# The last stick-breaking head feeds TensorE float32 values directly, without the split into a rounded and a low part

## What is computed

```python
z = einsum('bhqd,bhkd->bhqk', qb, kh[:, :, :end]) * scale
strict = s_pos < t_pos
log_beta = log_sigmoid(z)
log_1m = where(strict, -softplus(z), 0.0)
suffix = cumsum(log_1m, axis=3, reverse=True) - log_1m
a = where(strict, exp(log_beta + suffix), 0.0)
outs.append(einsum('bhqk,bhkd->bhqd', a, vh[:, :, :end]))
```

## Time and profile before

| | |
|---|---|
| median of 3 runs | 1202.79 us |
| the three runs | 1201.45, 1202.79, 1959.26 us |
| the profiled execution | 1201.39 us, span 1199.5 us |
| TensorE busy | 1161.3 us, 97% |
| DVE, ACT, POOL busy | 47%, 47%, 48% |

### The profile page before, as it was taken

One profiled execution on the slowest core, in us unless ns is written; L12 is line 12 of the kernel. 1 busy time (PEld: TensorE's weight loads), 2 busy tenths in 40 slices (PEclk: granted clock), 3 DMA queues, 4 the chain that ended last, 5 costly groups with the idle time before them and its releaser, 6 DMA issues.

```text
span 1199.5 us, 15304 instructions
## 1 busy us (share of the span) xinstructions
PE 1161.3 (97%) x5566; PEld 973.9 (81%) x5566; DVE 559.8 (47%) x760; ACT 569.7 (47%) x834; POOL 572.2 (48%) x292
## 2 busy tenths in 40 slices
PE   7999998989999999999999999899999999999996
PEld 5888887878888888888888889687888888888885
DVE  7756677766222222222455666768642222222225
ACT  5778887444233223133446878855331422322421
POOL 3535563574434444444644645447554444444450
PEclk9999998999999999999999999999999999999998
DMA  5212110322332323322221211112332232232322
GB/s 185 73 51 70 37 36 19 105 87 90 108 101 90 105 87 105 97 96 88 92 84 53 71 36 55 51 36 71 123 106 99 95 97 97 87 105 87 105 71 71
DMA packets 30153, 99.63 MB, mean 83 GB/s; under 512 B 3728, under 2 KB 5776, under 8 KB 30096
## 3 DMA queue, kind: packets, MB, share of 16 engines
q1 hardware_dynamic: 29664, 98.33, 24.7%
q10 hardware_dynamic: 432, 0.55, 0.1%
HBM read 96.77 MB, written 2.10 MB: 82 GB/s over the span
## 4 chain that ended last, share of the span: by engine, by line
PE 83%; ACT 4%; DVE 3%; issue 2%; POOL 2%; POOLq 2%; DMA 1%; DVEq 1%; SPq 0%; ACTq 0%
PE DW L418 23%; PE DW L420 23%; PE DW L419 23%; POOL w L905 2%; PE Z L563 2%; PE Z L570 2%; PE Z L552 1%; DMA raw<-in_weights 1%; PE DW L508 1%; PE O L582 1%; POOLq L913 1%; PE Z L418 1%; PE Z L420 1%; PE Z L419 1%; PE O L532 1%
## 5 line engine op out<-in xcount | busy, mean ns | idle before, releaser
L905 POOL TENSOR_TENSOR w<-raw,w 128x1024 fp32r<-128x1024 f32 x178 | 431.8, 2427 | 384.3 <-ACT w L675 380.0
L675 ACT ACTIVATE w<-raw 128x1024 fp32r<-128x1024 f32 x177 | 185.8, 1052 | 216.9 <-PE DW L420 195.6
L418 PE MATMUL DW<-xm,w 128*128 128x512 f32 x512 | 201.0, 393 | 5.1 <-POOL w L905 5.1
L420 PE MATMUL DW<-xm,w 128*128 128x512 f32 x512 | 199.9, 390 | 0.0
L419 PE MATMUL DW<-xm,w 128*128 128x512 f32 x512 | 199.8, 390 | 0.0
L418 PE MATMUL DW<-stage,w 128*128 128x512 f32 x512 | 199.5, 390 | 0.0
L420 PE MATMUL DW<-stage,w 128*128 128x512 f32 x512 | 199.2, 389 | 0.0
L419 PE MATMUL DW<-stage,w 128*128 128x512 f32 x512 | 199.2, 389 | 0.0
L1224 DVE TENSOR_TENSOR kf<-o 128x512 f32<-128x512 f32 x64 | 65.2, 1019 | 196.7 <-ACT o L856 196.5
L1240 DVE TENSOR_TENSOR DW<-DW,probs 128x512 f32<-128x512 f32 x62 | 43.4, 699 | 222.9 <-PE DW L420 222.9
L418 PE MATMUL DW<-xa,w 128*128 128x512 f32 x296 | 119.9, 405 | 7.8 <-DVE xa L1013 7.8
(11 more groups left out here) (216 smaller groups left out, 1644.5 us busy)
## 6 DMA issues: line engine op xcount, KB each, us to landing
raw<-in_weights SPq DMA_DIRECT2D x179, 512.0 KB, 3.3
out_x<-x SPq DMA_DIRECT2D x16, 128.0 KB, 1.9
x<-in_x SPq DMA_DIRECT2D x6, 256.0 KB, 6.3
raw<-in_weights SPq DMA_DIRECT2D x2, 256.0 KB, 4.8
x<-in_x ACTq DMA_DIRECT2D x2, 256.0 KB, 5.4
work<-in_positions SPq DMA_DIRECT2D x1, 256.0 KB, 6.8
gains<-in_gains ACTq DMA_DIRECT2D x1, 28.0 KB, 3.9
inv_freq<-in_inv_freq SPq DMA_DIRECT2D x1, 0.5 KB, 7.1
```

Source lines behind the costliest of these rows:

```text
L418: pe.matmul(bank, w[:, slot, 0, k], rhs[:, 0, c], start=start, stop=False)
L420: mm = pe.matmul(bank, w[:, slot, 1, k], rhs[:, 0, c], start=False, stop=stop)
L675: act.activation(w[:, slot_of(at_layer), 0], raw[:, p % 2], ACT.Identity).then_inc(w_hi, 1)
L905: pool.tensor_tensor(w[:, slot, 1], raw[:, p % 2], w[:, slot, 0].bitcast(F32), ALU.subtract).then_inc(w_ready, 1)
```

## The change

In head 7 alone, BX reads `work` itself as float32, once, in place of `sp` hi and lo, and BA reads `work` itself in place of `at` hi and lo. The constants and the values are read as float32 too. The steps BH7, BL7, XH7 and XL7 are gone, and the counts that other waits use are adapted (seven splits in a layer, not eight). BX7 now waits for BP7, and BA7 for XE7. A wait of BH7 for BX6 goes with it. Both order tables are written anew: in layer 1 almost only the four steps drop out, in layer 0 more of them stand in another place.

```diff
 BX:
-pe.wait_ge(sb_split, l * SB_HEADS + n + 1)
+if n == LAST_HEAD:
+    pe.wait_ge(sb_sp, l * SB_HEADS + n + 1)
+    parts = [work[:, n % 2]]
+    tri, one = minus_tri[:, :].bitcast(F32), minus_one[:, :].bitcast(F32)
+else:
+    pe.wait_ge(sb_split, l * SPLIT_HEADS + n + 1)
+    parts = [sp[:, 0], sp[:, 1]]
+    tri, one = minus_tri[:, :], minus_one[:, :]
 for j in (0, 1, 3, 2):
-    for f in range(2):
-        pe.matmul(Z[n][:, Z_AT[j]:Z_AT[j] + Z_LEN[j]], minus_tri[:, :],
-                  sp[:, f, Z_AT[j]:Z_AT[j] + Z_LEN[j]],
...
+    for part in parts:
+        pe.matmul(Z[n][:, Z_AT[j]:Z_AT[j] + Z_LEN[j]], tri, part[:, Z_AT[j]:Z_AT[j] + Z_LEN[j]],
...
 BA:
-pe.wait_ge(sb_alo, l * SB_HEADS + n + 1)
+if n == LAST_HEAD:
+    pe.wait_ge(z_drained, l * SB_HEADS + n + 2)
+    parts, v = [work[:, n % 2]], vst.bitcast(F32)
+else:
+    pe.wait_ge(sb_alo, l * SPLIT_HEADS + n + 1)
+    parts, v = [at[:, 0], at[:, 1]], vst
...
 BH:
 act.wait_ge(sb_sp, l * SB_HEADS + n + 1)
-if n == LAST_HEAD:
-    act.wait_ge(zx_full, l * SB_HEADS + n)
 act.activation(sp[:, 0], work[:, n % 2], ACT.Identity).then_inc(sb_hi, 1)
...
 ORDER_0, last lines:
-BP7 BH7 BD5 BL7 OS0 CH21 XH6 GH2 OS1 GL2 XL6 OS2 BX7 OE0 CL20 BA6 XE7 BO6 OS3 XH7 BD6 XL7 OE1 CL21 OE2 OS4
-CH22 CL22 BA7 BO7 OS5 BD7 CH23 OE3 CL23 GH3 CH24 CL24 OS6 OS7 NS0 GL3 NSE0 OE4 OE5 NSD0 NSF0 OE6 OE7
+BO5 BP7 OS1 BD5 CH21 GL1 GH2 XL6 OS2 BX7 OE0 CL20 OE1 BA6 XE7 BO6 OS3 BD6 BA7 OS4 CH22 OE2 CL21 CL22 BO7 BD7
+CH23 OE3 CL23 GH3 OS5 CH24 OS6 CL24 NS0 GL2 OE4 GL3 NSE0 OS7 OE5 NSD0 NSF0 OE6 OE7
```

More of the change, by code:

```diff
@@ L93 @@
 LAST_HEAD = SB_HEADS - 1
+SPLIT_HEADS = SB_HEADS - 1
 ORDER_0 = """
[L113 to L126, removed]
@@ L127 @@
-BP7 BH7 BD5 BL7 OS0 CH21 XH6 GH2 OS1 GL2 XL6 OS2 BX7 OE0 CL20 BA6 XE7 BO6 OS3 XH7 BD6 XL7 OE1 CL21 OE2 OS4
-CH22 CL22 BA7 BO7 OS5 BD7 CH23 OE3 CL23 GH3 CH24 CL24 OS6 OS7 NS0 GL3 NSE0 OE4 OE5 NSD0 NSF0 OE6 OE7
+T0 U0 AG0 T1 CH3 AG1 NP0 NA0 NAE0 AG2 NAD0 T2 AG3 CL3 NAF0 TE0 AG4 U1 AG5 AG6 TH0 AG7 CH4 U2 TL0 TE1 TE2 AG8
+CL4 AG9 CH5 T3 AG10 TH1 AG11 TL1 U3 RE2 CL5 SN0 RM2 TE3 T4 RS2 RE3 RA2 RS3 U4 TH2 RM3 T5 CH6 TL2 RA3 TE4 TH3
+CL6 VT4 VH4 TL3 CH7 BS0 BE0 U5 VL4 T6 TE5 RE5 BP0 CL7 RM5 RS5 U6 RA5 BH0 TH5 BL0 TE6 CH8 BX0 TL5 WS0 VT6 XE0
@@ new lines @@
+CH9 WM0 BS1 T7 WE0 CL8 VH6 WR0 WN0 WT0 U7 WH0 WL0 BE1 TE7 TH7 WS1 VL6 WM1 T8 U8 WE1 BP1 BH1 CH10 WR1 CL9 WN1
+WA0 XH0 WO0 XL0 TL7 TE8 BL1 WT1 WH1 T9 WL1 WS2 WD0 CH11 TH8 BX1 WA1 WM2 WE2 XE1 WO1 TL8 U9 WR2 WD1 CL10 WN2
+BS2 CL11 CH12 TE9 WT2 WH2 RE9 BA0 T10 WL2 RM9 BO0 RS9 WS3 BE2 BD0 RA9 TH9 WM3 U10 WA2 CL12 CH13 TL9 WE3 XH1
+T11 WO2 BP2 WR3 TE10 U11 BH2 RE10 BL2 WN3 RM10 RS10 XL1 TE11 CH14 RA10 TH10 WT3 BX2 CL13 VT11 SQ0 BA1 WH3 WD2
+SQ1 WL3 XE2 TL10 VH11 BO1 BS3 WS4 BD1 BE3 WM4 T12 WE4 CL14 WA3 WO3 U12 BP3 WR4 WN4 WT4 VL11 XH2 BH3 WH4 TE12
@@ new lines @@
+WD3 WL4 BL3 T13 WS5 CH15 WA4 XL2 WM5 CL15 TH12 BX3 WE5 TL12 WR5 U13 WO4 SA0 WN5 TE13 T14 CH16 WD4 WT5 XE3 TH13
+BA2 TL13 SQ2 BS4 WH5 CL16 SA1 WL5 WS6 XH3 BE4 WM6 BO2 XL3 WE6 BD2 CH17 BP4 T15 U14 SA2 WA5 BH4 WR6 TE14 U15
+BL4 SQ3 WN6 WT6 TH14 WO5 WH6 BX4 CH18 TE15 WD5 WL6 WS7 TL14 VT15 BA3 SQ4 XE4 WM7 BO3 BS5 BD3 T16 SA3 CL17 VH15
+SQ5 WE7 SA4 CL18 WA6 BE5 VL15 WO6 WR7 WN7 U16 WT7 WD6 T17 BP5 XH4 XL4 WH7 WL7 BH5 SQ6 SA5 BL5 WA7 TE16 SA6
+CH19 WO7 WD7 U17 CH20 TH16 TE17 GH0 BX5 GL0 SQ7 XE5 SA7 NW0 CL19 TL16 NWE0 NWD0 NWF0 BS6 MN0 BA4 BE6 MH0 MN1
@@ L129 @@
+MN2 VT17 BS7 GH1 BP6 BH6 ML0 XH5 MN3 MH1 VH17 BL6 MH2 BO4 VL17 BX6 XL5 BD4 MH3 BA5 ML1 ML2 BE7 XE6 ML3 XH6 OS0
+BO5 BP7 OS1 BD5 CH21 GL1 GH2 XL6 OS2 BX7 OE0 CL20 OE1 BA6 XE7 BO6 OS3 BD6 BA7 OS4 CH22 OE2 CL21 CL22 BO7 BD7
+CH23 OE3 CL23 GH3 OS5 CH24 OS6 CL24 NS0 GL2 OE4 GL3 NSE0 OS7 OE5 NSD0 NSF0 OE6 OE7
 """
@@ L143 @@
 XE5 NW0 NWE0 TL17 GH0 BS6 NWD0 CL20 BE6 GH1 NWF0 GL0 MN0 BA4 CH21 MN1 BP6 BH6 MH0 XH5 MN2 MH1 MN3 BO4 BS7 BL6
-ML0 XL5 BD4 MH2 ML1 MH3 BX6 ML2 BE7 ML3 BA5 OS0 XE6 OS1 BP7 BH7 OS2 BL7 OE0 GL1 XH6 BX7 XL6 BO5 OE1 OS3 BD5
-XE7 BA6 OE2 BO6 CL21 XH7 OS4 BD6 OE3 OS5 XL7 GH2 CH22 OE4 BA7 OS6 CL22 BO7 BD7 OE5 GH3 GL2 OS7 GL3 NS0 OE6
-CH23 CH24 NSE0 OE7 NSD0 CL23 CL24 NSF0
+ML0 XL5 BD4 MH2 ML1 MH3 BX6 ML2 BE7 ML3 BA5 OS0 XE6 OS1 BP7 OS2 OE0 GL1 XH6 BX7 XL6 BO5 OE1 OS3 BD5 XE7 BA6
+OE2 BO6 CL21 OS4 BD6 OE3 OS5 GH2 CH22 OE4 BA7 OS6 CL22 BO7 BD7 OE5 GH3 GL2 OS7 GL3 NS0 OE6 CH23 CH24 NSE0 OE7
+NSD0 CL23 CL24 NSF0
 """
@@ L558, in _ @@
                     elif step == "BX":
-                        pe.wait_ge(sb_split, l * SB_HEADS + n + 1)
+                        if n == LAST_HEAD:
[6 more added lines that the diff above has]
+                            tri, one = minus_tri[:, :], minus_one[:, :]
                         for j in (0, 1, 3, 2):
-                            for f in range(2):
-                                pe.matmul(Z[n][:, Z_AT[j]:Z_AT[j] + Z_LEN[j]], minus_tri[:, :],
-                                          sp[:, f, Z_AT[j]:Z_AT[j] + Z_LEN[j]],
-                                          start=False, stop=j == NB - 1 and f == 1, skip_group_check=True)
+                            for part in parts:
+                                pe.matmul(Z[n][:, Z_AT[j]:Z_AT[j] + Z_LEN[j]], tri, part[:, Z_AT[j]:Z_AT[j] + Z_LEN[j]],
+                                          start=False, stop=j == NB - 1 and part is parts[-1], skip_group_check=True)
                         for j in range(NB - 1):
@@ L568, in _ @@
                                 at0 = Z_AT[j] + P * (jj - j)
[L569 to L572, removed]
+                                for part in parts:
+                                    mm = pe.matmul(Z[n][:, at0:Z_AT[j] + Z_LEN[j]], one,
+                                                   part[:, Z_AT[jj]:Z_AT[jj] + Z_LEN[jj]], start=False,
+                                                   stop=jj == NB - 1 and part is parts[-1], skip_group_check=True)
                         mm.then_inc(zx_full, 1)
                     elif step == "BA":
-                        pe.wait_ge(sb_alo, l * SB_HEADS + n + 1)
+                        if n == LAST_HEAD:
[4 more added lines that the diff above has]
+                            parts, v = [at[:, 0], at[:, 1]], vst
                         pe.wait_ge(o_drained, l * O_USES + plan.o_use[step, n] + 1)
@@ L580, in _ @@
                         for j in range(NB):
[L581 to L584, removed]
+                            for part in parts:
+                                mm = pe.matmul(O[:, j * P:T], v[:, n // 2 % 2, j, n % 2, :],
+                                               part[:, Z_AT[j]:Z_AT[j] + Z_LEN[j]],
+                                               start=j == 0 and part is parts[0],
+                                               stop=j == NB - 1 and part is parts[-1])
                         mm.then_inc(o_full, 1)
@@ L782, in _ @@
                         if n > 1:
-                            act.wait_ge(sb_alo, l * SB_HEADS + n - 1)
+                            act.wait_ge(sb_alo, l * SPLIT_HEADS + n - 1)
                         act.activation(work[:, n % 2], Z[n], ACT.Abs)
@@ L1138, in _ @@
                     elif step == "BL":
-                        dve.wait_ge(sb_hi, l * SB_HEADS + n + 1)
+                        dve.wait_ge(sb_hi, l * SPLIT_HEADS + n + 1)
                         dve.tensor_tensor(sp[:, 1], work[:, n % 2], sp[:, 0].bitcast(F32), ALU.subtract
```

8 lines of the change are left out of this document (4 added, 4 removed).

## The result

The changed kernel takes 1204.4 us (median of 20 runs, 1203.31 to 1205.19), the kernel before 1201.49 us in runs on the same chip (median of 20, from 1199.7). The ratio is 1.0024, with a 95% interval of 1.0018 to 1.003: about 2.9 us slower. One run of the kernel before took 1959.26 us; it is left out of the comparison, and what delayed it isn't known. The profiled execution of the changed kernel took 1203.89 us.

The account below looks back on a forecast made before the run. TensorE, busy 1161.3 of 1199.5 us, was taken as the bound. Layer 1's +2.5 and layer 0's -0.6 us gave 1203.3 us on the profiled 1201.39, 1204.7 on the median 1202.79; forecast 1204 us, 8-in-10 range 1199.5 to 1208.5.

Parts of the forecast that it names:

- Removed steps, zero: Head 7's four split steps on ACT, DVE and POOL: removing them ends no TensorE wait, zero, at most 1.6 us.
- Float32 products, +2.5 us a layer: BX7 and BA7 on TensorE: at 1.68 ns a column they grow by 1.58 and 0.94 us in each layer.
- The dear end for small products: 128-column float32 products in BX7 and BA7 might each cost as much as 256-column ones: 1.1 us more.
- Layer 1, +2.5 us, rigid: Layer 1 behind BA7: everything moves by 2.5 us, and the 1.94 us pause ahead of the MLP stays.
- Layer 0, -0.6 us, as 1.0 - 1.56: Layer 0: MLP starts 1.0 us later, pause shrinks from 3.13 to 1.6 us, and a kept-up clock saves 1.56 us.
- The pause of 1.94 us doesn't drop the clock, that of 3.13 us does: TensorE's clock behind the pause ahead of the MLP: with 1.6 us, layer 0 should match layer 1, saving 1.56 us.
- The early reorder of layer 0, zero with 1.6 us to either side: The other rearranged steps of ORDER_0: short groups change places where TensorE hardly waits, zero, bounds 1.6 us either way.
- Rival 1: Layer 0's pause absorbs nothing, pack 26 moves with TensorE, clock falls: 1206.4 or 1207.8 us, up to 1209; chance 0.24.
- Rival 2: Layer 0's new order removes the short waits and the clock stays up: 1200 to 1202.5 us; chance 0.16.
- Rival 3: A float32 product on TensorE costs only what the two parts cost, so no added work: 1198.2 us; chance 0.03.
- The signs of being wrong: 128-column float32 products far above 0.21 us, a changed wait of BX6, or a new wait in the first 180 us.

Follow-up runs that it names:

- the first experiment: The changed kernel's float32 arithmetic for head 7, in the order tables of the kernel before less the four steps: 1207.18 us, ratio 1.0046 against the kernel before.

## Why the prediction was right, and where it wasn't

The forecast of 1204 us met 1204.4, but that is closer than its sum was. The sum is a difference of +1.9 us, and +2.9 was measured (2.2 to 3.6). The rest is the base. I put the forecast between a sum on 1201.39 us and one on 1202.79. The second base is the median of three runs, one of them at 1959.26 us, and lies 1.3 us above the 1201.49 of twenty runs. That part of the hit is luck. Taken by its steps:

- **Removed steps, zero.** Right. The wait before BX6 is 4.98 us as before, none of the removed steps ended a wait, and the run with the old order shows nothing saved by them: its +5.5 us are the products' 2 x 2.40 and 0.7 us more. What the term lacked is that their absence can cost. I saw that XL7 stood ahead of packs 21 and 22 and their DMAs, and asked only whether TensorE waits for a pack. In the old order pack 23 came early, stood beside BD7 on DVE, and OS7 waited 0.51 us for DVE. The changed order has no such wait.
- **Float32 products, +2.5 us a layer.** Right: 2.40 us. The slope of 1.68 ns a column held down to 128 columns, and slightly better: 4.26 us over 2560 columns is 1.66, 2.07 us over 1280 is 1.62. The dear end for small products didn't occur. A float32 product of 512 columns takes 0.86 us from start to start and one of fp32r 0.23, 3.8 times less. The four passes that the Trainium skill gives for true FP32 (page "FP8 and Floating Point Precision", section "TensorE Precision Notes") fit that. Its half rate for FP32_LOW_HIGH (page "Perfetto Trace Analysis", section "Engine Utilization") isn't the price of these products; the page doesn't say of which it is.
- **Layer 1, +2.5 us, rigid.** Right: +2.62 at the MLP and +2.63 at the end, with the pause unchanged at 1.95 us. The 0.2 us between 2.40 and 2.62 stand ahead of BX7: the way from BX6 to BX7 took 14.53 us instead of 14.25, which is less than it varies with the clock behind BX6 (last section).
- **Layer 0, -0.6 us, as 1.0 - 1.56.** The mechanism was right in its first half. NSF's last operation took 0.69 us, d0 left at 230.47 (expected 231.3), DVE waited for TensorE from there, the pause shrank to 1.38 us (expected 1.6), the twelfth product came 2.63 us after the first (expected 2.7). Two terms were mis-sized. The MLP started 0.30 us sooner and not 1.0 later. Of this, 0.2 us is the pause and 0.1 the products, both a little under the forecast, and 0.9 us is that TensorE was back at its upper clock sooner behind BX6: BX7 started at 205.09 instead of 206.00, ahead of every changed product. The wait at BX6 was the same, and the stretch behind it varies between executions by as much (last section). The second is a term the prediction lacked: the low parts of `xm`. I read pack 26's start on POOL and TensorE's wait for it, but not which DVE operation then stands beside pack 26. In the new timing it was a low part of `xm`, held for 2.96 us, then the next one beside pack 27, and 1.73 us of TensorE's gain went there. The sum was -0.14 us instead of -0.6. The two errors had opposite signs.
- **The pause of 1.94 us doesn't drop the clock, that of 3.13 us does.** Right for the two executions, wrong as a rule. See the last section. In the term it was a certain 1.56 us; it should have been an expectation of part of it.
- **The early reorder of layer 0, zero with 1.6 us to either side.** Held. NS0 in the kernel before stood at 225.10, in the changed one at 223.83: -1.27 us. That is -0.91 + 2.40 - 2.74 (one tile) = -1.25, so as a sum nothing is left for the rest of the order. It isn't idle all the same: by the first experiment the old order would have cost 0.7 us here.
- **The rivals.** Rival 1 was real, with the old order: 1207.18 us was measured for it where 1206.4 to 1207.8 was worked out. Rival 2 asked for short waits to vanish; they didn't. Rival 3 falls by BX7's 4.26 us.
- **The signs of being wrong.** One of them showed, a new wait in the first 180 us: 0.93 us at 19.36, where the kernel before waits 0.2, and 0.42 us at 45.26. The first isn't from the new order, since the old-order kernel has 0.73 us in the same place, and both cost little: BX6 starts 0.11 us later than before.

Beside the base, layer 0 is the place where the hit was partly luck: 0.9 us of clock in one execution stands against 1.7 us of waits for `xm`.

## What to carry to other kernels

Before a split into rounded and low part is dropped, look for who waits for it: at head 7 nobody did, and plain float32 products cost 2.4 us a layer; at head 6 TensorE waited 5 us for it, and the float32 form of BX alone gained 3.4 us over both layers. An operation that is taken off POOL moves the ones behind it, so look at what they will stand beside as well: in the old order that went with 0.7 us lost. Where a pause ahead of a stage shrinks, the inputs after the first are next: list the operations that make them, and which operation of POOL each will newly stand beside. A delay on the bounding engine passes through in full unless a pause behind it absorbs it, and whether it does is decided by where the chain behind that pause starts.
